# SBUF layout by size, one table for exp and ln, and a 64-byte shift between two weight rings

## The chip, the cores and the metric

The kernel runs on one core of one Trainium2 chip. The metric is the device time of the whole kernel in microseconds (us). The kernel before takes 2155.08 us, the median of 3 runs (2154.45 to 2155.72).

## The reference

The reference is a decoder trunk of two layers over 256 tokens of width 2048, float32. Each layer has a mixer and a feed-forward block:

```python
h = rmsnorm(x, g_norm) @ w_in                       # 2048 -> 3072: q, k, v of 4 + 4 heads of 128
o_sb  = stick_breaking(rmsnorm(qa), rmsnorm(ka), va)
o_dil = dilated_attention(rope(rmsnorm(qb)), rope(rmsnorm(kb)), vb)
x = x + concat([rmsnorm(o_sb), rmsnorm(o_dil)]) @ w_out
x = x + ffn(rmsnorm(x))       # layer 0: dense SwiGLU, d_ff 5632; layer 1: top-2 of 8 experts, 1408 each
```

Stick-breaking attention needs log1p(exp(z)) of the scores and later an exp of the result; dilated attention is a masked softmax, computed here as one softmax with a count per key. So each head needs both exp and ln.

## The kernel before, in words

The 256 tokens are two tiles of 128 (t = 0, 1). Every large product is made of float32r matmuls in three parts. A weight is split in a high part (rounded to float32r) and a low part (the rest), and so is the activation; the product is high x high + high x low + low x high, added up in PSUM. Activations are the stationary operand (128 columns), weights the moving one (mostly 512 columns, 256 in the last gate/up block of a feed-forward slice). The function `three` issues them: L417 has w_high moving, L418 w_low moving, both against the high part of the activation, and L419 has w_high moving against its low part.

Weights arrive in pieces of 128 x 1024 floats (512 KB) through a ring of 11 slots. SyncE loads a piece into raw_pieces (L320) when the slot is free; ScalarE copies it, rounded, to w_high (L748); VectorE writes raw minus high to w_low (L997), which has the same addresses as raw_pieces; TensorE then uses it. ScalarE and VectorE work 6 pieces ahead (LEAD), 14 in the expert stage. There are 96 pieces for w_in and 32 for w_out over both layers, 264 for the dense block and 528 for the experts.

The stages follow one another in each layer. The input projection and the gate and up products have xT_high and xT_low (the normalised, transposed activation) as stationary operands. The output projection and the down products have hT_high and hT_low (the transposed attention output, or the transposed hidden activation). In the expert stage only 128 gathered tokens are used per expert (t = 0 alone); gathers (L659) and scatters (L673, L674, with selection_T stationary) lie among the products.

The order of work on each engine is written out by hand, with semaphores between engines. Between the input and the output projection lies the attention stage, in which no weight piece is used. For each head ScalarE evicts and scales transposed q and k (L810, L811, L814), copies the scores z (L822) and their absolute value (L823), computes exp(-|z|) (L825) and ln(1 + ...) (L826), then exp for the softmax (L829, L830), then exp for the stick-breaking weights (L836). VectorE computes row maxima of the dilated scores (L1133 to L1136), then from the ln the softplus and its masks (L1139 to L1143), then multiplies the softmax terms by the counts (L1146) and sums them (L1148, L1149, L1150), and then forms the exponent of the stick-breaking weights (L1156 to L1158) from TensorE's suffix sums (L500 to L502). In one head VectorE does them in this order, and TensorE the scores of the next head (L484 to L491) after the suffix sums of this one.

ScalarE's functions come from table sets. The program gets a table load (ACT_TABLE_LOAD) ahead of an activation whose function is not in the set that is loaded. exp and ln alternate in every head; sqrt is used before and after the attention stage (L772); Copy, Abs and Square never cause a load here between others.

SBUF tensors are laid out one behind the other in the order in which they are declared; raw_pieces, mixer_scratch and heads_scratch share the addresses of the tensors declared after them. In the kernel before, the order and the bytes per partition are: w_low 45,056; w_high 45,056; x_resid 16,384; token_major 24,576; xT_high 16,384; xT_low 16,384; silu_gate 4096; h_blocks 4096; identity, incl, ones, neg_not_strict, keep_strict 512 each; branch_count and neg_union 1536 each; rope_cos, rope_sin, router_high, router_low 512 each; expert_gates 64; small 256; hT_high 11,264; hT_low 11,264; and behind them small tensors and iota_slots 512, selection 1024, selection_T 1024.

Of the kernel before, what the change touches and what calls it, by code (L numbers as in the profile page):

```python
# [6 lines left out]
F32 = mybir.dt.float32  # L7
F32R = mybir.dt.float32r
# [5 lines left out]
P = 128  # L14
SEQ = 256
TILES = SEQ // P
# [9 lines left out]
FC = FE // P  # L26
# [62 lines left out]
SLOTS = P  # L89
# [34 lines left out]
def trunk(nc, x, positions, norm_mix, w_in, q_norm_sb, k_norm_sb, q_norm_dil, k_norm_dil, out_norm_sb,  # L124
# [36 lines left out]
    with ExitStack() as ctx:  # L161
        def sb(name, shape, dt=F32, where=ctx):
            return where.enter_context(nc.sbuf_tensor(name, shape, dt))
# [4 lines left out]
        with ExitStack() as scratch:  # L168
            RAWS = sb("raw_pieces", [P, RING, PW], F32, scratch)
        WL = sb("w_low", [P, RING, PW], F32R)  # L170
        WH = sb("w_high", [P, RING, PW], F32R)
        X = sb("x_resid", [P, TILES, D])
        TOK = sb("token_major", [P, TILES * D_IN])

# [1 line left out]
            ATT = sb("mixer_scratch", [P, 2 * KD * SEQ], F32, scratch)  # L176
        XTH = sb("xT_high", [P, KD, SEQ], F32R)
        XTL = sb("xT_low", [P, KD, SEQ], F32R)
        SG = sb("silu_gate", [P, 2 * TILES, GW])
        HB = sb("h_blocks", [P, 2, TILES, GW])  # L180
        IDN = sb("identity", [P, P])
# [3 lines left out]
        KEEPZ = sb("keep_strict", [P, P])  # L185
        CNT = sb("branch_count", [P, 3 * P])
        NEGU = sb("neg_union", [P, 3 * P])
        COS = sb("rope_cos", [P, TILES, DH // 2])
        SIN = sb("rope_sin", [P, TILES, DH // 2])
        WRH = sb("router_high", [P, KD, N_EXP], F32R)  # L190
# [3 lines left out]
        XN = TOK[:, 0:TILES * D].rearrange("p (t n) -> p t n", t=TILES)  # L194
        GAIN = TOK[:, TILES * D:TILES * D + D]
        QKV = TOK[:, :].rearrange("p (t n) -> p t n", t=TILES)

        with ExitStack() as scratch:
            PRE = sb("heads_scratch", [P, 2 * FC * SEQ], F32, scratch)
        HTH = sb("hT_high", [P, FC, SEQ], F32R)  # L200
        HTL = sb("hT_low", [P, FC, SEQ], F32R)


        at = [0]
# [26 lines left out]
        SSP = sb("block_square_sums", [P, TILES * DBLOCKS])  # L231
        JUNK = SG[:, :, :].rearrange("p t n -> p (t n)")[:, 0:NB]
        SB_GAIN = SMALL[:, 4:6]
# [7 lines left out]
        R1 = sb("router_rows", [P, 4, TILES, N_EXP])  # L241
        CHOSEN = sb("chosen", [P, TILES, N_EXP])
        SLOT = sb("slot", [P, TILES, N_EXP])
        IOTA = sb("iota_slots", [P, SLOTS])
        SEL = sb("selection", [P, TILES, SLOTS])
        LGT = SEL[:, :, :].rearrange("p t s -> p (t s)")[0:N_EXP, :]
        SELT = sb("selection_T", [P, SEQ], F32R)
        FLAG = sb("another_pass", [P, 1], I32)
        YH = [HTH[:, 4 * i:4 * i + 4, P:2 * P] for i in range(2)]
        YL = [HTL[:, 4 * i:4 * i + 4, P:2 * P] for i in range(2)]  # L250
# [62 lines left out]
        def _(sp):  # L313
# [13 lines left out]
            for t in range(TILES):  # L327
                sp.dma_start(X[:, t, :], x[t * P:(t + 1) * P, :]).then_inc(x_in[t], 16)
            for layer in range(LAYERS):
# [15 lines left out]
            for d in range(DBLOCKS):  # L345
                for t in range(TILES):
                    sp.wait_ge(sc_free, 2 + last + TILES * d + t + 1)
                    sp.dma_start(out[t * P:(t + 1) * P, d * NB:(d + 1) * NB],
                                 X[:, t, d * NB:(d + 1) * NB]).then_inc(stored, 16)
            sp.wait_ge(stored, 16 * DBLOCKS * TILES)  # L350
# [62 lines left out]
        def _(pe):  # L413
# [22 lines left out]
            def both_tiles(banks, act, k, slot, lo, width, first, last):  # L436

                for t in range(TILES):
                    ins = three(banks[t][:, 0:width], act, (slice(None), k, slice(t * P, (t + 1) * P)),
                                (WH, WL), (slice(None), slot, slice(lo, lo + width)), first, last)  # L440
                return ins

            pe.wait_ge(const_done, 1)
            for layer in range(LAYERS):
# [4 lines left out]
                for c in range(IN_BLOCKS):  # L449
# [4 lines left out]
                    for j in range(IN_PIECES):  # L454
                        n = m["p_in"] + c * IN_PIECES + j
                        pe.wait_ge(low_done, n + 1)
                        for u in range(2):
                            k = 2 * j + u
                            ins = both_tiles(PAIR[c % 2], (XTH, XTL), k, n % RING, u * NB, NB, k == 0, k == KD - 1)
                        ins.then_inc(used, 1)  # L460
# [98 lines left out]
                if layer == 1:  # L559
                    pe.wait_ge(wr_done, 1)  # L560
                    for k in range(KD):
                        ks = (slice(None), k, slice(None))
                        ins = three(DN[0][0:N_EXP, 0:SEQ], (WRH, WRL), ks, (XTH, XTL), ks, k == 0, k == KD - 1)
                    ins.then_inc(lgt_ready, 1)
# [7 lines left out]
                def ffn_slice(e):  # L572
# [12 lines left out]
                    for i in range(SLICE_PIECES):  # L585
                        n = f["piece"] + i
                        if i < GU_PIECES:
# [6 lines left out]
                            for k, lo in units:  # L594
                                ins = both_tiles(PAIR[b % 2], (XTH, XTL), k, n % RING, lo, 2 * gu_width(b), k == 0,
                                                 k == KD - 1)
# [29 lines left out]
            def moe_pass(n_pass):  # L626
                s = PASS[n_pass]

                def piece_products(bnk, act, k, slot, lo, width, first, last):
                    return three(bnk[:, 0:width], act, (slice(None), k, slice(0, SLOTS)), (WH, WL),  # L630
                                 (slice(None), slot, slice(lo, lo + width)), first, last)

                def gate_up(e, i):
# [6 lines left out]
                    for k, lo in units:  # L640
                        ins = piece_products(G[b % 2], (XTH, XTL), k, n % RING, lo, 2 * gu_width(b), k == 0, k == KD - 1)
                    ins.then_inc(used, 1)
# [94 lines left out]
        def _(act):  # L737
# [7 lines left out]
            def high(piece, shift=0):  # L745

                act.wait_ge(raw_full[piece % RING], shift * (16 * SLICE_PIECES // RING) + 16 * (piece // RING + 1))
                act.activation(WH[:, piece % RING, :], RAWS[:, piece % RING, :], ACT.Copy).then_inc(high_done, 1)  # L748

            n_square = [0]  # L750

            def squares(d, t):

                act.wait_ge(sq_done, n_square[0]) if n_square[0] else None
                n_square[0] += 1
                act.activation(JUNK, X[:, t, d * NB:(d + 1) * NB], ACT.Square,
                               accum_out=SSP[:, DBLOCKS * t + d:DBLOCKS * t + d + 1]).then_inc(sq_done, 1)
# [21 lines left out]
            for layer in range(LAYERS):  # L779
# [11 lines left out]
                for c in range(IN_BLOCKS):  # L791
# [5 lines left out]
                    if c in QK_BLOCKS:  # L797
                        n = QK_BLOCKS.index(c)
                        roots(HSSR[:, 8 * n:8 * n + 8], ROOTS * layer + 1 + n)

                act.wait_ge(sbg_done, layer + 1)

                def turned(h):
# [182 lines left out]
        def _(dve):  # L986
# [7 lines left out]
            def low(piece, shift=None):  # L994

                dve.wait_ge(high_done, piece + 1 if shift is None else shift * SLICE_PIECES + (piece + 1))
                dve.tensor_tensor(WL[:, piece % RING, :], RAWS[:, piece % RING, :], WH[:, piece % RING, :],  # L997
                                  ALU.subtract).then_inc(low_done, 1)
# [7 lines left out]
            def normalise(norm):  # L1006

                dve.wait_ge(sq_done, X_BLOCKS * (norm + 1))
                link(dve.tensor_reduce(SS, SSP[:, :].rearrange("p (t d) -> p t d", t=TILES), AX.X, ALU.add))
                inverse_roots(RSTD, SS, D, ROOTS * (norm // 2) + (ROOTS - 1) * (norm % 2))  # L1010
                dve.wait_ge(xg_done, X_BLOCKS * (norm + 1))

            def times_gain(d, t):

                cols = slice(d * NB, (d + 1) * NB)
                dve.tensor_tensor(XN[:, t, cols], X[:, t, cols], GAIN[:, cols], ALU.mult).then_inc(xg_done, 1)

# [16 lines left out]
            def x_low(k, t, q):  # L1034
                dve.wait_ge(tp_high, k + 1)
                dst = (slice(None), slice(4 * q, 4 * q + 4), slice(t * P, (t + 1) * P))
                dve.tensor_tensor(XTL[dst], TP[k % 2][:, :].rearrange("p (c n) -> p c n", c=4), XTH[dst],  # L1037
                                  ALU.subtract).then_inc(tp_free, 1)
# [38 lines left out]
            for layer in range(LAYERS):  # L1077
# [17 lines left out]
                def heads_normalised(c):  # L1095
# [5 lines left out]
                    link(dve.tensor_tensor(SQ, cols, cols, ALU.mult))  # L1101
                    link(dve.tensor_reduce(sums, SQ.rearrange("p t (h d) -> p (t h) d", d=DH), AX.X, ALU.add))
                    inverse_roots(rs, sums, DH, ROOTS * layer + 1 + n)
# [175 lines left out]
            def moe_pass(n_pass):  # L1279
# [12 lines left out]
                def gathered_low(high_count, k, q):  # L1292
                    dve.wait_ge(tp_high, high_count + 1)
                    dst = (slice(None), slice(4 * q, 4 * q + 4), slice(0, SLOTS))
                    dve.tensor_tensor(XTL[dst], TP[k % 2][:, :].rearrange("p (c n) -> p c n", c=4), XTH[dst],
                                      ALU.subtract).then_inc(tp_free, 1)
# [131 lines left out]
```

## Time and profile before

| | |
|---|---|
| median of 3 runs | 2155.08 us |
| the profiled execution's own time | 2153.96 us |
| its span in the trace | 2152.2 us |
| TensorE busy | 2036.9 us (95%) |
| VectorE busy | 1426.2 us (66%) |
| ScalarE busy | 1166.0 us (54%) |
| HBM traffic | 492 MB, 229 GB/s over the span |

The profile is of one execution. Matmuls are pipelined and the records of two neighbours overlap, so a busy TensorE is not one at its peak; the distance between the starts of two matmuls is the rate. The granted clock tells which level the throttle allows TensorE: 1.0 is 2.4 GHz, 0.5 is 1.2 GHz. The stages lie, in us from the start of the span, at about: input projection of layer 0 to 166, attention to 221, output projection to 268, dense block 286 to 1053, input projection of layer 1 to 1180, attention to 1233, output projection and routing to 1330, experts to the end.

### The profile page before, as it was taken

To read this page: it belongs to the slowest core of one execution; us is meant where nothing else is said; L and a number is where in the kernel's file an instruction comes from. 1 tells how busy PE (TensorE), PEld (TensorE's weight loads), DVE (VectorE), ACT (ScalarE), POOL (GpSimd) and SP (SyncE) were. 2 spreads that over 40 slices of the span, in tenths; PEclk is the share of its full clock that TensorE was granted. 3 is DMA by queue.
4 is the path that set the end of the run, shared out by engine and by line. 5 is a ranking of instruction groups with operands and counts; after the bars stand their busy time and mean duration, and the time that the engine had idled before them with its cause. 6 is when DMAs were issued, how large, how long until landed. Compare 5 with 4: busy or idle time off the path is not lost.

```text
span 2152.2 us, 28336 instructions
## 1 busy us (share of the span) xinstructions
PE 2036.9 (95%) x9604; PEld 1686.8 (78%) x9604; DVE 1426.2 (66%) x1714; ACT 1166.0 (54%) x1460; POOL 13.5 (1%) x35
## 2 busy tenths in 40 slices
PE   5995989999999999999899688999999999999998
PEld 4884778888888887888687567888888888888886
DVE  7564554544454454446556566888989898989896
ACT  5437443443443443434434734777777776767675
POOL 1000000000000000000000000000000000000000
PEclk9998989999999999999899798999999999999999
DMA  6551445555555555555355044989898998989896
GB/s 226 191 193 39 166 147 187 186 188 194 186 186 189 193 185 187 187 186 188 128 195 186 22 156 159 359 313 347 320 341 322 336 335 320 345 315 354 306 359 251
DMA packets 135270, 493.54 MB, mean 229 GB/s; under 512 B 15264, under 2 KB 15264, under 8 KB 134400
## 3 DMA queue, kind: packets, MB, share of 16 engines
q1 hardware_dynamic: 133920, 486.60, 63.4%
q0 software_dynamic: 1248, 5.61, 0.8%
q8 instruction: 61, 1.00, 0.2%
q14 instruction: 41, 0.34, 0.0%
HBM read 490.05 MB, written 2.10 MB: 229 GB/s over the span
## 4 chain that ended last, share of the span: by engine, by line
PE 91%; ACT 4%; DVE 3%; issue 1%; DMA 0%; DVEq 0%; ACTq 0%; POOLq 0%
PE main L417 28%; PE main L419 28%; PE main L418 28%; PE transpose L659 3%; PE transpose L424 1%; PE spread L673 1%; PE spread L674 1%; DVE xT_low L1037 1%; PE transpose L699 1%; ACT L826 0%; PE transpose L581 0%; DMA token_major<-in_norm_mix 0%; ACT w_high L748 0%; ACT xT_high L767 0%; DVE w_low L997 0%
## 5 line engine op out<-in xcount | busy, mean ns | idle before, releaser
L997 DVE TENSOR_TENSOR w_low<-raw_pieces,w_high 128x1024 fp32r<-128x1024 f32 x920 | 1087.9, 1219 | 432.7 <-ACT w_high L748 420.5
L748 ACT ACTIVATE w_high<-raw_pieces 128x1024 fp32r<-128x1024 f32 x920 | 933.2, 1056 | 259.9 <-DMA raw_pieces<-in_ffn_dense 135.4
L417 PE MATMUL main<-w_high,xT_high 128*128 128x512 f32 (+1 forms) x1920 | 730.3, 380 | 5.5 <-DVE xT_low L1037 4.5
L419 PE MATMUL main<-w_high,xT_low 128*128 128x512 f32 (+1 forms) x1920 | 723.1, 377 | 0.0
L418 PE MATMUL main<-w_low,xT_high 128*128 128x512 f32 (+1 forms) x1920 | 722.7, 376 | 0.0
L417 PEld LDWEIGHTS main<-w_high,xT_high 128*128 128x128 f32 x1920 | 363.0, 189 | 73.1 <-issue 4.3
L419 PEld LDWEIGHTS main<-w_high,xT_low 128*128 128x128 f32 x1920 | 362.8, 189 | 66.3
L418 PEld LDWEIGHTS main<-w_low,xT_high 128*128 128x128 f32 x1920 | 363.4, 189 | 64.1
L417 PE MATMUL main<-w_high,hT_high 128*128 128x512 f32 x832 | 333.8, 401 | 2.8 <-DVE hT_low L1180 2.8
L418 PE MATMUL main<-w_low,hT_high 128*128 128x512 f32 x832 | 329.8, 396 | 0.0
L419 PE MATMUL main<-w_high,hT_low 128*128 128x512 f32 x832 | 329.6, 396 | 0.0
L417 PEld LDWEIGHTS main<-w_high,hT_high 128*128 128x128 f32 x832 | 157.3, 189 | 39.3 <-DVE hT_low L1180 3.6
L419 PEld LDWEIGHTS main<-w_high,hT_low 128*128 128x128 f32 x832 | 156.9, 189 | 38.1
L418 PEld LDWEIGHTS main<-w_low,hT_high 128*128 128x128 f32 x832 | 157.2, 189 | 35.4
L908 ACT ACTIVATE silu_gate<-main 128x256 f32<-128x256 f32 (+1 forms) x48 | 15.0, 364 | 210.3 <-PE main L419 210.3
L1187 DVE TENSOR_TENSOR x_resid<-main,x_resid 128x512 f32<-128x512 f32 x48 | 31.9, 687 | 120.6 <-PE main L419 120.6
L424 PE MATMUL transpose<-identity,token_major 128*128 128x128 f32 x160 | 40.5, 424 | 56.7 <-DVE token_major L1021 31.0
L424 PEld LDWEIGHTS transpose<-identity,token_major 128*128 128x128 f32 x160 | 29.2, 216 | 67.5 <-issue 29.1
L954 ACT ACTIVATE hT_high<-main 128x512 fp32r<-128x512 f32 x32 | 19.2, 599 | 100.2 <-PE main L419 100.2
L796 ACT ACTIVATE token_major<-main 128x512 f32<-128x512 f32 x24 | 13.0, 595 | 100.6 <-PE main L419 100.6
L659 PEld LDWEIGHTS transpose<-selection,token_major 128*128 128x128 f32 x512 | 63.8, 198 | 4.2 <-DVEq L1240 1.6
L659 PE MATMUL transpose<-selection,token_major 128*128 128x128 f32 x512 | 64.2, 281 | 1.6 <-DVEq L1240 1.6
(203 smaller groups left out, 883.4 us busy)
## 6 DMA issues: line engine op xcount, KB each, us to landing
raw_pieces<-in_ffn_moe SPq DMA_DIRECT2D x528, 512.0 KB, 5.1
raw_pieces<-in_ffn_dense SPq DMA_DIRECT2D x264, 512.0 KB, 3.4
raw_pieces<-in_w_in SPq DMA_DIRECT2D x96, 512.0 KB, 4.3
raw_pieces<-in_w_out SPq DMA_DIRECT2D x32, 512.0 KB, 4.2
x_resid<-in_x SPq DMA_DIRECT2D x2, 1024.0 KB, 7.0
token_major<-in_norm_mix POOLq DMA_DIRECT2D x2, 1024.0 KB, 7.2
token_major<-in_norm_ffn POOLq DMA_DIRECT2D x2, 1024.0 KB, 5.0
out_x<-x_resid SPq DMA_DIRECT2D x8, 256.0 KB, 2.7
```

The costliest lines, as they stand in the source:

```text
L417: pe.matmul(out_ap, lh[ls], rh[rs], start=first, stop=False)
L418: pe.matmul(out_ap, lh[ls], rl[rs], start=False, stop=False)
L419: return pe.matmul(out_ap, ll[ls], rh[rs], start=False, stop=last)
L424: ins = pe.transpose(TP[k % 2][:, i * P:(i + 1) * P], src[:, c * P:(c + 1) * P], IDN[:, :])
L659: ins = pe.matmul(TP[k % 2][:, i * P:(i + 1) * P], XN[:, t, c * P:(c + 1) * P], SEL[:, t, :], start=t == 0, stop=t == TILES - 1)
L673: pe.matmul(bnk, rows, YH[d % 2], start=True, stop=False)
L674: pe.matmul(bnk, rows, YL[d % 2], start=False, stop=True).then_inc(sc_ready, 1)
L699: ins = pe.transpose(TP[n % 2][:, c * P:(c + 1) * P], HB[:, b % 2, 0, c * P:(c + 1) * P], IDN[:, :])
L748: act.activation(WH[:, piece % RING, :], RAWS[:, piece % RING, :], ACT.Copy).then_inc(high_done, 1)
L997: dve.tensor_tensor(WL[:, piece % RING, :], RAWS[:, piece % RING, :], WH[:, piece % RING, :], ALU.subtract).then_inc(low_done, 1)
L1037: dve.tensor_tensor(XTL[dst], TP[k % 2][:, :].rearrange("p (c n) -> p c n", c=4), XTH[dst], ALU.subtract).then_inc(tp_free, 1)
L1187: dve.tensor_tensor(xs, PAIR[d % 2][t][:, :], xs, ALU.add).then_inc(dn_free, 1)
```

## The change

It does three things. Large SBUF tensors (hT, and the selection tensors) are declared ahead of the small ones. A pad of 64 bytes stands between w_low and w_high, and one of 448 bytes behind w_high. And ahead of each attention stage ScalarE loads one table set, named natural_log_exp_and_others. Nothing else of the program changes.

```diff
         WL = sb("w_low", [P, RING, PW], F32R)
+        PAD = sb("ring_shift", [P, P // 8])
         WH = sb("w_high", [P, RING, PW], F32R)
+        PAD2 = sb("ring_shift_back", [P, P - P // 8])
         X = sb("x_resid", [P, TILES, D])
...
         XTL = sb("xT_low", [P, KD, SEQ], F32R)
+        with ExitStack() as scratch:
+            PRE = sb("heads_scratch", [P, 2 * FC * SEQ], F32, scratch)
+        HTH = sb("hT_high", [P, FC, SEQ], F32R)
+        HTL = sb("hT_low", [P, FC, SEQ], F32R)
         SG = sb("silu_gate", [P, 2 * TILES, GW])
...
         NEGU = sb("neg_union", [P, 3 * P])
+        SEL = sb("selection", [P, TILES, SLOTS])
+        SELT = sb("selection_T", [P, SEQ], F32R)
+        IOTA = sb("iota_slots", [P, SLOTS])
         COS = sb("rope_cos", [P, TILES, DH // 2])
...
-        with ExitStack() as scratch:
-            PRE = sb("heads_scratch", [P, 2 * FC * SEQ], F32, scratch)
-        HTH = sb("hT_high", [P, FC, SEQ], F32R)
-        HTL = sb("hT_low", [P, FC, SEQ], F32R)
...
-        IOTA = sb("iota_slots", [P, SLOTS])
-        SEL = sb("selection", [P, TILES, SLOTS])
         LGT = SEL[:, :, :].rearrange("p t s -> p (t s)")[0:N_EXP, :]
-        SELT = sb("selection_T", [P, SEQ], F32R)
...
                         roots(HSSR[:, 8 * n:8 * n + 8], ROOTS * layer + 1 + n)
 
+                act.preload_act_table_set("natural_log_exp_and_others")
                 act.wait_ge(sbg_done, layer + 1)
```

## Rows read from the trace of the kernel before

**Rows 1.** The page: busy time by engine, and the chain's shares by engine.
```profile
PE 2036.9 (95%) x9604; PEld 1686.8 (78%) x9604; DVE 1426.2 (66%) x1714; ACT 1166.0 (54%) x1460; POOL 13.5 (1%) x35
...
PE 91%; ACT 4%; DVE 3%; issue 1%; DMA 0%; DVEq 0%; ACTq 0%; POOLq 0%
```

**Rows 2.** TensorE's waits, 1345 to 2140: us in total, times, longest.
```profile
PE transpose L699 <- DVE h_blocks L1322: 2.5, 8, 0.3
```

**Rows 3.** The windows view: stretch, us, busy (instructions) per engine, PEclk, DMA share, GB/s.
```profile
1345.00:2140.00 795.00, 792.47 (x3905) 661.17 (x3904) 695.37 (x744) 567.78 (x655) 0.00 (x0) 1.00 0.91 332
```

**Rows 4.** Timeline of TensorE, xT stationary: start us, us, engine, line, operation. 26 rows between.
```profile
157.70 0.39 PE L418 MATMUL main<-w_low,xT_high 128*128 128x512 f32 x1
...
163.82 0.39 PE L418 MATMUL main<-w_low,xT_high 128*128 128x512 f32 x1
```

**Rows 5.** The same, hT stationary: output projection (28 rows between), experts (9 between).
```profile
228.15 0.40 PE L418 MATMUL main<-w_low,hT_high 128*128 128x512 f32 x1
...
234.92 0.39 PE L417 MATMUL main<-w_high,hT_high 128*128 128x512 f32 x1
...
1484.19 0.40 PE L418 MATMUL main<-w_low,hT_high 128*128 128x512 f32 x1
...
1486.53 0.40 PE L419 MATMUL main<-w_high,hT_low 128*128 128x512 f32 x1
```

**Rows 6.** The page's groups: counts of L417, with xT and with hT.
```profile
L417 PE MATMUL main<-w_high,xT_high 128*128 128x512 f32 (+1 forms) x1920 | 730.3, 380 | 5.5 <-DVE xT_low L1037 4.5
...
L417 PE MATMUL main<-w_high,hT_high 128*128 128x512 f32 x832 | 333.8, 401 | 2.8 <-DVE hT_low L1180 2.8
```

**Rows 7.** Timeline of TensorE at 1.2 GHz, right after attention. Three rows between.
```profile
222.19 0.63 PE L418 MATMUL main<-w_low,hT_high 128*128 128x512 f32 x1
...
223.89 0.63 PE L419 MATMUL main<-w_high,hT_low 128*128 128x512 f32 x1
```

**Rows 8.** Timeline of ScalarE, head 0 of layer 0.
```profile
165.84 1.08 ACT L796 ACTIVATE token_major<-main 128x512 f32<-128x512 f32 x2 [8.15 <-PE main L419]
166.81 0.48 ACT L810 ACTIVATE mixer_scratch<-transpose,small 128x256 f32<-128x256 f32 x1
...
169.55 1.28 ACT L825 ACT_TABLE_LOAD   x1
```

**Rows 9.** L1139's waits in 8 heads (us, times), and timeline rows of VectorE and ScalarE.
```profile
  ACT mixer_scratch L826: 13.0, 8
...
182.75 0.56 DVE L1139 SCALAR_TENSOR_TENSOR mixer_scratch<-mixer_scratch 128x384 f32<-128x384 f32 x1 [0.84 <-ACT mixer_scratch L826]
...
184.34 0.49 ACT L830 ACTIVATE mixer_scratch<-mixer_scratch,small 128x256 f32<-128x256 f32 x1
184.54 0.28 DVE L1143 TENSOR_TENSOR mixer_scratch<-mixer_scratch,keep_strict 128x128 f32<-128x128 f32 x1
...
1192.65 0.56 DVE L1139 SCALAR_TENSOR_TENSOR mixer_scratch<-mixer_scratch 128x384 f32<-128x384 f32 x1 [0.66 <-ACT mixer_scratch L826]
...
1210.35 0.56 DVE L1139 SCALAR_TENSOR_TENSOR mixer_scratch<-mixer_scratch 128x384 f32<-128x384 f32 x1 [0.93 <-ACT mixer_scratch L826]
```

**Rows 10.** Groups of ScalarE: table loads in attention, count | busy us, mean ns | idle before.
```profile
L826 ACT ACT_TABLE_LOAD x8 | 10.3, 1283 | 0.1
L829 ACT ACT_TABLE_LOAD x8 | 10.3, 1283 | 0.1
...
L825 ACT ACT_TABLE_LOAD x2 | 2.6, 1283 | 0.0
```

**Rows 11.** Timeline of TensorE, 256 columns: router (3 rows between), then main (19 between).
```profile
1299.83 0.28 PE L418 MATMUL main<-xT_low,router_high 128*8 128x256 f32 x1
...
1300.30 0.28 PE L419 MATMUL main<-xT_high,router_low 128*8 128x256 f32 x1
...
1479.79 0.28 PE L417 MATMUL main<-w_high,xT_high 128*128 128x256 f32 x1
...
1482.19 0.28 PE L419 MATMUL main<-w_high,xT_low 128*128 128x256 f32 x1
```

## The prediction

> **What bounds the kernel now.** I read the page's busy shares and chain first. TensorE is busy for 2036.9 of 2152.2 us and carries 91% of the chain that ended last; ScalarE has 4% of it and VectorE 3% [rows 1]. So only two things can move the end: how fast TensorE goes through its matmuls, and the stretches in which it does nothing. The waits of TensorE in the expert stage (1345 to 2140) come next: 2.5 us in 795 [rows 2]. This stage moves the most bytes, but the DMA share is 0.91 at 332 GB/s [rows 3], and TensorE never waits there for a weight piece. The kernel is TensorE-bound from end to end, outside the two attention stages.
>
> Since matmuls overlap, their mean duration says nothing of the rate; the distance from one start to the next does, so the timeline is the view that matters. With xT as the stationary operand, 27 matmuls of 512 columns go by between 157.70 and 163.82: 6.12/27 = 226.7 ns each [rows 4]. With hT as the stationary operand, in the output projection, 29 go by between 228.15 and 234.92: 233.4 ns; in the expert stage 10 between 1484.19 and 1486.53: 234 ns [rows 5]. Shape, width, clock level (2.4 GHz, granted clock 1.0) and moving operand (w_high, w_low) are the same. At 2.4 GHz, 512 columns alone are 213.3 ns, so each matmul carries 13.4 ns (xT) or 20 ns (hT) on top. While the clock was granted at 1.2 GHz, four took 1.70 us, 425 ns each [rows 7], which is 512 columns and nothing on top.
>
> **What the layout may have to do with it.** By the allocation order and sizes of the kernel before, and counting from w_low, w_high lies 45,056 bytes further, xT_high 131,072, xT_low 147,456: all whole multiples of 512 bytes. hT_high comes after two small tensors of 64 and 256 bytes and lies 180,032 bytes after w_low, which is 351 x 512 + 320; hT_low has the same remainder. A slice of 128 columns is 512 bytes, a ring slot 4096, so the remainder holds for every operand of these matmuls. This remainder is the one thing in which I find hT to differ from xT, in two stages with different loops, and in both the distance is 6.7 ns greater. I take it as the cause. Both rows come with the weight load of the next matmul beside the running one, so I read the excess as the two reads getting into each other's way.
>
> The Trainium skill (TensorE: Matmul & The Clock Gate, the pipeline's first step, LDWEIGHTS) says that TensorE has two independent SBUF read ports and that loading the next weights doesn't steal read bandwidth from the running matmul. By that rule the layout is worth nothing. The trace speaks against it: the same instruction forms go at two rates. I go by the trace and keep the rule's outcome as rival C.
>
> **Part 1, the layout by size.** hT_high, hT_low, selection, selection_T and iota_slots move ahead of the small tensors. With both pads together 512 bytes, x_resid, token_major and xT keep their remainder of 0, and hT_high gets it too: it lies 163,840 + 512 = 164,352 bytes after w_low, 321 x 512. No instruction is added or removed. The stationary hT then stands to w_low as xT does, and I take xT's distance for it: 3 x 832 = 2496 matmuls [rows 6] x (233.3 - 226.7 = 6.6 ns) = 16.5 us, all on TensorE and so all on the path. Bounds: 0, if the remainder is not the cause; the saving could be larger if selection_T, whose remainder becomes 0 too, speeds up the 128 scatter matmuls (at 7 ns, under 1 us). DMA hides none of it: of the 832 groups of three, 352 are in the expert stage, so some 7 us of its 795 go, and the DMA share of 0.91 would rise by 0.01.
>
> **Part 2, the 64-byte shift.** All of w_high, the moving operand of L417 and L419 (two of every three matmuls), now has remainder 64, while w_low and all stationary operands have 0. No row of before shows a remainder of 64. On the low side there is a bound: the router's matmuls of 256 columns with only 8 stationary columns to load go 0.47/4 = 117.5 ns apart, against 2.40/20 = 120 ns for the main ones of that width [rows 11], so some 2.5 ns per matmul are what a whole weight load costs beyond a nearly empty one. If the shift took that away from all 3 x (1920 + 832) = 8256 matmuls, it would give 20.6 us. Above: if remainder 64 is as bad as 320, L417 and L419 pay 6.6 ns: 5504 x 6.6 = 36.3 us lost. The far end, no excess at all as at 1.2 GHz, would be 8256 x 13.4 = 110 us; nothing at 2.4 GHz comes near it. The splits on ScalarE and VectorE also read and write the rings; TensorE doesn't wait for them, so a small change in them is hidden by TensorE's own time. I take 0 between 20.6 gained and 36.3 lost, since rows give no sign, and the zero is the weakest term of the sum.
>
> **Part 3, one table.** Table loads of 1283 ns: 8 at L826 (ln), 8 at L829 (back to exp), 2 at L825 (exp after the square root) [rows 10]. With a set holding both functions all 18 go, and 2 come, ahead of the wait on sbg_done. Is the new load hidden? No: ScalarE's two evictions run to 166.92 and L810 starts at once (166.81, the two overlap a little); the load pushes L810, the score matmuls and all after it back by 1.28 us. It takes the place of the load at 169.55, which was on the chain as well [rows 8]. These cancel: 0 (bounds: 1.28 us each way, per layer).
>
> The load at L826 stands before the ln whose result L1139 waits for. VectorE's idle time before L1139 is 13.0 us in 8 heads; removing a load gives at most 1.28 us of each wait. Three waits are shorter, 0.84, 0.66 and 0.93 [rows 9], because VectorE's row-maximum work, which comes after TensorE's scores, ends later than the ln without its load would; the other five give 1.28. Sum 5 x 1.28 + 2.43 = 8.8 us. The load at L829 feeds L1146 by way of L830. In head 1 of layer 0 VectorE starts L1139 at 182.75 and is busy until L1143 ends at 184.82; L830 ends at 184.83 [rows 9]. Both arrive together, so removing this load alone gives nothing: VectorE's five operations are late next. Worth 0 (bounds: 0 and 8 x 1.28 = 10.3 us). Behind it, ScalarE's evictions come earlier, but no one is late for them. In the same rows the instruction after a load starts 0.01 us after its end: the Trainium skill (ScalarE: Activation LUTs, What ACT_TABLE_LOAD costs) adds a drain of 1380 ns to each switch; the trace doesn't show it. With it the part would be worth about twice as much.
>
> TensorE's clock: the granted clock is 1.2 GHz at times in the attention stages and for six matmuls after them [rows 7]. Shorter idle time may shift these stretches either way; six matmuls at 1.2 GHz cost 6 x 0.2 = 1.2 us, so I allow 2 us each way.
>
> **The sum**, on the profiled execution (2153.96 us, 1.76 more than its span): -16.5 + 0 - 8.8 = -25.3, so 2128.7; the median of the runs is 1.1 us above it: 2129.8. I say 2130.
>
> **Rivals.**
> A, the forecast: rings as now, hT as xT: 2130. Its own range is 2119 to 2139 (the clock, part of a shift gain, a part of hT's excess that stays).
> B, the shift costs. Two of three matmuls get hT's 6.6 ns: -25.3 + 36.3 = +11: 2166. For it: hT, 320 bytes off, shows that a ring and a stationary operand at unequal remainders can be slow; a shift makes L417 and L419 unequal. If the reads repeat over 128 bytes, 320 and 64 are the same thing. Against: three matmuls in a row may settle otherwise than when all have one remainder. The result turns slower once the shift costs more than 25.3/5504 = 4.6 ns per shifted matmul.
> C, layout without effect (the two rates have another cause): 2155.1 - 8.8 = 2146. Against: two stages, same difference.
> D, the shift helps: up to 20.6 us more, 2109. For it: reads that start in different places need not meet. Then the expert stage would come closer to DMA: its share of 0.91 at 332 GB/s would rise by about the same part as TensorE gets faster, under 2%, so the end still follows TensorE.
> E, the table pass still loads for ln or exp: 8.8 us less gain, 2139, or 2155 with C.
>
> **How the numbers follow.** A 0.45, B 0.22, C 0.10, D 0.18, E 0.05. The time is A's. Range 2109 to 2164: it takes in D almost whole, A, C, E and the milder half of B; outside it remain a B at full price or worse and a D beyond its bound, together about 0.18. About 0.2% (4.3 us) is what a measurement of this kernel can tell. Faster: A, C, D, E and a mild B, 0.80; within 0.2%: 0.04; slower: 0.16.
>
> **What would show it.** Starts of matmuls with hT 226.7 ns apart instead of 233.4 confirm part 1; 233.4 unchanged mean C. With xT: 226.7 is A, less is D, 231 on average over a group of three is B. Table loads at L825, L826 and L829 gone, one per layer ahead of L810, idle before L1139 down from 13.0 to about 4 us confirm part 3; loads at L826 still there mean E. The forecast is wrong if xT's distance moves by over 2 ns either way.

## The result, and the profile after

The changed kernel takes 2168.68 us (median of 6 runs, 2166.31 to 2172.36) against 2154.17 us for the kernel before (6 runs): ratio 1.0068, 95% interval 1.0055 to 1.0081. It is slower by 14.5 us, where 2130 was forecast. Rival B, the shift that costs, had been worked out at 2166. Every ratio in this document is to the kernel before as run beside the other kernel, and one execution stands in no ratio: of the three of e5_shift_128 one took 10,066.52 us, while the others took 2142.95 and 2143.90.

The distances between matmul starts tell it. These are timeline rows of TensorE in the changed kernel (start us, us, engine, line), with xT stationary; 23 rows lie between the first and the last. They answer to [rows 4]; `three` is one line further down, L418 to L420, since a line was added above it.

```profile
99.71 0.40 PE L418 MATMUL main<-w_high,xT_high 128*128 128x512 f32 x1
99.94 0.40 PE L419 MATMUL main<-w_low,xT_high 128*128 128x512 f32 x1
100.18 0.39 PE L420 MATMUL main<-w_high,xT_low 128*128 128x512 f32 x1
...
105.31 0.40 PE L418 MATMUL main<-w_high,xT_high 128*128 128x512 f32 x1
```

5.60/24 = 233.3 ns, where it was 226.7. With hT stationary, in the output projection (23 rows between), answering to [rows 5]:

```profile
231.63 0.40 PE L418 MATMUL main<-w_high,hT_high 128*128 128x512 f32 x1
...
237.23 0.40 PE L418 MATMUL main<-w_high,hT_high 128*128 128x512 f32 x1
```

Again 5.60/24 = 233.3 ns, as before. So xT got slower and hT gained next to nothing: its mean distance is 233.4 ns in the dense block, 232.6 in the experts and 231.0 in the second output projection, where it was 233.3 in all of them. The page shows the busy shares of [rows 1] hardly changed, and the table loads of ScalarE (groups: count, busy us, mean ns, idle before) are what part 3 promised: the 18 of [rows 10] are gone, and two stand at L802.

```profile
PE 2060.9 (95%) x9604; PEld 1684.4 (78%) x9604; DVE 1426.7 (66%) x1714; ACT 1145.1 (53%) x1444; POOL 13.5 (1%) x35
...
PE 92%; DVE 4%; ACT 3%; issue 1%; DMA 0%; DVEq 0%; ACTq 0%; POOLq 0%
```

```profile
L802 ACT ACT_TABLE_LOAD x2 | 2.6, 1283 | 0.0
```

The table below is worked out from the starts of the first and the last main matmul of each stage (us; attention from the last xT matmul to the first hT one; the last line counts matmuls of every kind). Two experiments, told below, stand beside the two kernels.

| stage | before | after | e1_no_shift | e2_table_only |
|---|---|---|---|---|
| input projection, layer 0 | 132.1 | 137.0 | 132.5 | 131.9 |
| attention, layer 0 | 56.2 | 50.1 | 51.1 | 51.4 |
| output projection, layer 0 | 46.0 | 46.1 | 45.8 | 46.5 |
| dense block | 742.3 | 752.7 | 735.0 | 739.7 |
| input projection, layer 1 | 132.5 | 136.3 | 132.1 | 132.5 |
| attention, layer 1 | 55.8 | 48.6 | 51.3 | 51.5 |
| output projection, layer 1 | 46.4 | 46.0 | 45.5 | 46.8 |
| experts | 824.6 | 834.2 | 819.6 | 824.6 |
| norms, routing, end | 92.4 | 92.6 | 93.8 | 92.6 |
| first to last matmul | 2128.3 | 2143.6 | 2106.7 | 2117.5 |

Before to after: the stages with weight matmuls take 28.4 us more, the attention stages 13.2 us less. The extra time is xT's: 4992 matmuls of 512 columns at some 6.1 ns more are 30 us; the 768 of 256 columns went the other way, from 119.8 to 118.8 ns, 0.8 us less. TensorE still does not wait for weights in the expert stage (1345 to 2140; us in total, times, longest), as in [rows 2]:

```profile
PE transpose L700 <- DVE h_blocks L1324: 2.6, 8, 0.3
```

### The profile page after: what moved, and what is told of

Read it like the earlier page. It is cut to its first block, busy times and chain, and to the rows that moved or that the text cites. A ratio compares the mean times of both kernels' runs of the same rounds, so it can differ in the third digit from the quotient of the medians.

```text
span 2166.9 us, 28320 instructions
## 1 busy us (share of the span) xinstructions
PE 2060.9 (95%) x9604; PEld 1684.4 (78%) x9604; DVE 1426.7 (66%) x1714; ACT 1145.1 (53%) x1444; POOL 13.5 (1%) x35
## 4 chain that ended last, share of the span: by engine, by line
PE 92%; DVE 4%; ACT 3%; issue 1%; DMA 0%; DVEq 0%; ACTq 0%; POOLq 0%
PE main L418 28%; PE main L419 28%; PE main L420 28%; PE transpose L660 3%; PE transpose L425 1%; PE spread L674 1%; PE spread L675 1%; DVE xT_low L1039 1%; PE transpose L700 1%; PE transpose L582 0%; DMA token_major<-in_norm_mix 0%; ACT w_high L749 0%; ACT xT_high L768 0%; DVE w_low L999 0%; DVE token_major L1018 0%
## 5 line engine op out<-in xcount | busy, mean ns | idle before, releaser
L749 ACT ACTIVATE w_high<-raw_pieces 128x1024 fp32r<-128x1024 f32 x920 | 933.4, 1056 | 265.5 <-DMA raw_pieces<-in_ffn_dense 137.7
L418 PE MATMUL main<-w_high,xT_high 128*128 128x512 f32 (+1 forms) x1920 | 741.9, 386 | 4.7 <-DVE xT_low L1039 4.5
L419 PE MATMUL main<-w_low,xT_high 128*128 128x512 f32 (+1 forms) x1920 | 735.0, 383 | 0.0
L420 PE MATMUL main<-w_high,xT_low 128*128 128x512 f32 (+1 forms) x1920 | 729.3, 380 | 0.0
L418 PEld LDWEIGHTS main<-w_high,xT_high 128*128 128x128 f32 x1920 | 361.4, 188 | 82.7 <-DVE xT_low L1039 3.6
L420 PEld LDWEIGHTS main<-w_high,xT_low 128*128 128x128 f32 x1920 | 364.1, 190 | 75.4
L419 PEld LDWEIGHTS main<-w_low,xT_high 128*128 128x128 f32 x1920 | 363.7, 189 | 71.9
L418 PE MATMUL main<-w_high,hT_high 128*128 128x512 f32 x832 | 334.6, 402 | 2.8 <-DVE hT_low L1182 2.8
L419 PE MATMUL main<-w_low,hT_high 128*128 128x512 f32 x832 | 330.4, 397 | 0.0
L420 PE MATMUL main<-w_high,hT_low 128*128 128x512 f32 x832 | 328.5, 395 | 0.0
L418 PEld LDWEIGHTS main<-w_high,hT_high 128*128 128x128 f32 x832 | 156.9, 189 | 39.5 <-DVE hT_low L1182 3.6
L420 PEld LDWEIGHTS main<-w_high,hT_low 128*128 128x128 f32 x832 | 157.6, 189 | 37.4
L419 PEld LDWEIGHTS main<-w_low,hT_high 128*128 128x128 f32 x832 | 157.5, 189 | 34.7
```

Of the source, the lines that this page charges most:

```text
L418: pe.matmul(out_ap, lh[ls], rh[rs], start=first, stop=False)
L419: pe.matmul(out_ap, lh[ls], rl[rs], start=False, stop=False)
L420: return pe.matmul(out_ap, ll[ls], rh[rs], start=False, stop=last)
```

## The experiments

**The change taken apart.** Four kernels: the changed kernel without its pads, and each of the three parts alone on the kernel before.

```diff
 e1_no_shift, against the changed kernel; e4_layout_only also drops the preload
-        PAD = sb("ring_shift", [P, P // 8])
-        PAD2 = sb("ring_shift_back", [P, P - P // 8])
 e2_table_only, against the kernel before
+                act.preload_act_table_set("natural_log_exp_and_others")
                 act.wait_ge(sbg_done, layer + 1)
 e3_shift_only, against the kernel before
+        PAD = sb("ring_shift", [P, P // 8])
         WH = sb("w_high", [P, RING, PW], F32R)
+        PAD2 = sb("ring_shift_back", [P, P - P // 8])
```

> The changed kernel without its two pads: layout by size and the one table stay. Theory 1 (the forecast's mechanism for hT, and the shift as the cost): every operand has remainder 0, so matmuls start 226.7 ns apart with xT and with hT alike; 2154 - 13 (attention stages, as in the changed kernel) - 16.5 (hT) = about 2125 us. Rival 2 (hT's 233.3 ns is not from its remainder): hT stays at 233.3 ns, 2141 us. Rival 3 (the slow xT comes from the moved tensors, not from the shift): xT stays at 233.3 ns, about 2167 us.

Measured: 2129.45 us (4 runs, 2128.02 to 2131.77), ratio 0.9885 (0.9869 to 0.9902). The timeline of TensorE, xT and then hT stationary, with 23 rows between in each pair:

```profile
109.76 0.39 PE L417 MATMUL main<-w_low,xT_high 128*128 128x512 f32 x1
...
115.20 0.39 PE L417 MATMUL main<-w_low,xT_high 128*128 128x512 f32 x1
...
235.67 0.39 PE L416 MATMUL main<-w_high,hT_high 128*128 128x512 f32 x1
...
241.11 0.39 PE L416 MATMUL main<-w_high,hT_high 128*128 128x512 f32 x1
```

5.44/24 = 226.7 ns in both. Theory 1 holds in the distances, rivals 2 and 3 fall: hT's extra time did come from its place, and xT's new slowness comes from the pads. The total is 4 us above theory 1's 2125, which had counted on the 13 us that the changed kernel gained in the attention stages; here these are 9.6 us shorter than before. This is the version that beats both kernels, by 24 us and 39 us.

> The kernel before with the one table load per layer alone. Theory 1 (the table is worth more than the 8.8 us of the forecast, because TensorE's clock in the attention stages recovers too): the two attention stages get 13 us shorter together, 2141 us, and xT and hT stay at 226.7 and 233.3 ns. Rival 2 (part of the 13 us comes from the layout, by way of the attention stages' own reads): 8.8 us, 2145 us.

Measured: 2142.31 us, ratio 0.9946 (0.9930 to 0.9963). xT stays at 226.7 ns, hT at 233.3. The two attention stages are 9.0 us shorter together, from 111.9 to 102.9. That is rival 2's number for the attention stages, and the forecast's 8.8, not theory 1's 13. Rival 2's reason is not shown by it: e1_no_shift has the layout too, and its attention stages take 102.4. Of the 11.5 us in the medians another 2.5 are in the dense block, where no instruction changed. The starts in the two traces tell where. The block begins at 1.2 GHz, for 5.7 us before and 3.2 here (granted clock of its first 10 us: 0.72 and 0.84), and after 15 matmuls 1.1 us of the difference is there. The other 1.4 us are three steps at the ends of its slices, where hT gives way to xT: before, the largest steps from start to start there are 0.68 and 1.08 us, here none is over 0.45. Why the clock rose earlier and the pauses went is open; no edit lies near them. The changed kernel's further 4 us in attention are taken up below.

> The kernel before with the two pads alone (w_high at remainder 64, hT at 320 as before, two tables as before). Theory 1 (the shift costs xT 6.6 ns and the attention stages nothing): xT at 233.3 ns, + 29 us in the input projections, gate and up products; hT stands to w_high at another remainder, which nobody has measured: if it stays at 233.3 ns, 2183 us; if it moves to the fast value, 2167 us. Rival 3 (the slow xT comes from the moved tensors): xT at 226.7 ns, 2154 us.

Measured: 2173.90 us, ratio 1.0091 (1.0074 to 1.0108). xT: mean distances of 231.1 ns in the first input projection and 233.3 in the dense block, the second projection and the experts; hT 229.1 in both layers' output projection and 230.4 in the experts. Neither of theory 1's totals came (2183 and 2167), since hT went to neither of its two values. The shift costs by itself; with hT at remainder 320 it even helps hT by 4 ns, so that what counts is a relation between two operands and not the remainder of one. This fits what the next experiments find: w_high then stands 64 - 320 = -256 bytes from hT, and only w_low is still at -320. The parts don't add up either: layout, table and shift alone make -10.9, -11.5 and +20.1 us, together -2.3, where the changed kernel with all three has +14.5. On the layout of before the shift slows xT and speeds hT up; on the layout by size it slows both.

> The kernel before with the layout by size alone. Theory 1: xT and hT at 226.7 ns, two tables in attention: 2154 - 16.5 = 2137.5 us. Rival 2 (remainders don't matter for hT): 2154 us.

Measured: 2142.94 us, ratio 0.9948 (0.9932 to 0.9965). hT at 226.9 ns, the attention stages as long as before (56.3 us each). The layout alone gives 10.9 us, against 16.5 in the expectation: the distances are as expected in every stage, but some stretches give part of it back (the input projections are 1.4 us longer together and the routing 1.0), and in the experts hT's mean is 227.6, since each gather and scatter between the down products disturbs the row for a few matmuls.

**Which relation counts.** Eight more kernels, all with the layout by size and the one table. By the relation of a matmul is meant the place of its moving operand minus the place of its stationary one, in bytes.

```diff
 e5_shift_128, e6_shift_256, e7_shift_32: the changed kernel with other pads, 512 bytes together
-        PAD = sb("ring_shift", [P, P // 8])
+        PAD = sb("ring_shift", [P, 32])        # 64 in e6, 8 in e7
-        PAD2 = sb("ring_shift_back", [P, P - P // 8])
+        PAD2 = sb("ring_shift_back", [P, 96])  # 64 in e6, 120 in e7
 e8_both_64: PAD of 16 floats ahead of raw_pieces and w_low instead of between the rings
 e9_both_192 and e10_both_128: the same with 48 and 32 floats (PAD2 of 80 and 96)
 e11_act_low_64, against e1_no_shift, and the same for HTL (the two scratch tensors get 128 floats more);
 e12_act_low_128 with 32 and 96
+        PAD = sb("low_shift", [P, 16])
         XTL = sb("xT_low", [P, KD, SEQ], F32R)
+        PAD2 = sb("low_shift_back", [P, 112])
```

> The changed kernel with w_high shifted by 128 instead of 64 bytes (and 384 behind it). Theory 1a (the reads meet by their place within 128 bytes): as without a shift, 226.7 ns with xT and hT, about 2130 us. Theory 1b (by their place within 512 bytes): another distance than 226.7 ns, up to hT's 233.3 ns and 2168 us.

> The same with 256 bytes. Theory 1a: 226.7 ns, 2130 us. Theory 1b: another distance; if the two reads are now as far from each other as they can be, a shorter one, down to 224 ns, 2108 us.

> The same with 32 bytes. If whole 64-byte lines count (theory 1a), 32 bytes lie in the same line at the start but cross into the next one in the middle of each: between 226.7 and 233.3 ns, some 230 ns, 2149 us. If only shifts of a whole 64 bytes matter: 226.7 ns, 2130 us.

> Both rings shifted by 64 bytes against the activations, and so equal among themselves; 448 bytes behind w_high. Theory A (what counts is moving against stationary operand, as hT with 320 bytes shows): 233.3 ns with xT and hT, 2166 us. Rival (what counts is w_high against w_low, whose reads follow one another): 226.7 ns, 2130 us.

> Both rings shifted by 192 bytes against the activations (320 behind them). Moving minus stationary is then 192, which modulo 256 is the relation that hT has in the kernel before (0 - 320 = -320 = 192 modulo 256). Theory P (the place within 256 bytes, moving against stationary, sets the distance): 233.3 ns with xT and hT alike, the rest as e1_no_shift, 2129 + 5760 x 6.6 ns + 2496 x 6.6 ns = about 2183 us, less if the 256-column ones gain as in the run before. Rival (that both rings are shifted doesn't matter, 64 bytes cost by the start of the ring): 229 ns as with both at 64, 2143 us.

> The same with 128 bytes, half of the 256 after which the shift of w_high alone came back to 226.7 ns. Theory P1 (two reads half the period apart meet least): below 226.7 ns, down to 224, 2108 us. Theory P2 (the fast value is the floor, and remainders other than 0 only add): between 226.7 and 233.3 ns, 2130 to 2183 us.

> Rings unshifted; the low halves of the activations (xT_low, hT_low, the stationary operands of one matmul in three) 64 bytes further. Theory P2: one relation in three leaves 0, so 226.7 ns rises to between 228 and 231 ns, 2140 to 2165 us. Theory P1' (a stagger can help when only one of three has it): below 226.7 ns, under 2125 us.

> The same with 128 bytes. Theory P2: as with w_high shifted by 128 (229 ns), but for one matmul in three: 227.5 to 229 ns, 2133 to 2143 us. Theory P1': below 226.7 ns, under 2125 us.

Measured, with the mean distance in the dense block (512 columns, xT and hT):

| kernel | moving minus stationary, bytes | xT ns | hT ns | us | ratio (95%) |
|---|---|---|---|---|---|
| e1_no_shift | 0 | 227.0 | 226.9 | 2129.45 | 0.9885 (0.9869 to 0.9902) |
| e6_shift_256 | w_high 256, w_low 0 | 227.0 | 226.9 | 2131.73 | 0.9892 (0.9864 to 0.9921) |
| e5_shift_128 | w_high 128, w_low 0 | 229.0 | 228.9 | 2143.90 | 0.9950 (0.9922 to 0.9979) |
| e8_both_64 | both 64 | 229.0 | 229.0 | 2143.38 | 0.9950 (0.9928 to 0.9973) |
| e11_act_low_64 | w_high against the low activation -64, the others 0 | 231.0 | 231.1 | 2154.75 | 1.0001 (0.9990 to 1.0013) |
| e12_act_low_128 | w_high against the low activation -128, the others 0 | 231.2 | 231.2 | 2157.06 | 1.0013 (1.0001 to 1.0024) |
| e7_shift_32 | w_high 32, w_low 0 | 231.2 | 231.1 | 2156.58 | 1.0014 (1.0003 to 1.0025) |
| e10_both_128 | both 128 | 232.5 | 232.4 | 2165.91 | 1.0055 (1.0032 to 1.0078) |
| the changed kernel | w_high 64, w_low 0 | 233.3 | 233.4 | 2168.68 | 1.0068 (1.0055 to 1.0081) |
| e9_both_192 | both 192 | 233.3 | 233.3 | 2169.69 | 1.0076 (1.0047 to 1.0106) |

One pair of rows each (xT stationary, 23 rows between) shows the fast and the slow end of the table, e6_shift_256 and then e9_both_192:

```profile
109.81 0.39 PE L418 MATMUL main<-w_high,xT_high 128*128 128x512 f32 x1
...
115.25 0.39 PE L418 MATMUL main<-w_high,xT_high 128*128 128x512 f32 x1
```

```profile
109.72 0.39 PE L420 MATMUL main<-w_high,xT_low 128*128 128x512 f32 x1
...
115.32 0.39 PE L420 MATMUL main<-w_high,xT_low 128*128 128x512 f32 x1
```

5.44/24 = 226.7 ns and 5.60/24 = 233.3 ns. What follows:
- A shift of w_high by 256 bytes gives what 0 gives, one of 128 doesn't (229.0 ns). Both have 512 bytes of pads like the changed kernel, so it is not the pads' size. Theory 1a, a period of 128 bytes, falls; nor does 1b's further hope, that the largest distance is the best, hold. A shift of 32 bytes gives 231.2 ns, where some 230 had been expected, and is slower than one of 128: the cost doesn't grow with the shift.
- e9 puts xT into the relation that hT has in the kernel before (0 - 320 = -320, which is 192 modulo 256), and xT takes hT's 233.3 ns. It takes hT's rhythm too: by the starts in the traces, xT's distances here and hT's before mostly alternate between 236 and 231 ns, where the changed kernel reaches the same mean as 232, 233, 240, 230, 234 and 231. So it is more than two slow values that happen to agree. Together with e1 and e4 this makes the places of the moving and the stationary operand relative to each other the cause of [rows 5]. What was not run is a kernel with rings and activations all shifted alike, which by this should be as fast as e1. The expected total of 2183 was 13 us too high: it put 6.6 ns on the 768 matmuls of 256 columns too, and they went from 119.8 down to 115.5 ns, which makes 8.4 us of it.
- e8 rules out its rival in its strict form: two equal rings are not enough, they must stand right to the activations. Its expected 233.3 ns was wrong too: both at 64 give 229.0 and not what both at 192 give. The relation is not symmetric.
- Theories P1 and P1', that some stagger does better than 0, fall for every shift in the table; 0 and 256 are the best, for matmuls of 512 columns. P2, that other relations only add, holds, and e10 and e11 came within its ranges. One was missed: e12 was expected at 227.5 to 229 ns and 2133 to 2143 us and came at 231.2 ns and 2157.06 us. One matmul in three at -128 costs more than two in three at 128 (229.0 ns, e5).
- With one of the three matmuls of a group off 0 (e11), the mean over the group is 231.0 ns (229, 229 and 236 in the starts of the input projection), 13 ns more for the three; with all three off by 64 the other way it is 229.0, 7 ns more. So the costs of single matmuls don't add up. Nor does the relation of each matmul say it all: -64 is 192 modulo 256, and with w_low alone at that relation (e3, hT in the output projections) the mean is 229.1 ns, with w_high against the low activation alone at it (e11) 231.0.

## Why the prediction was wrong, step by step

**What bounds the kernel: right.** TensorE alone set the end outside attention. Most of each change of the distances showed up in the stages' times, in the experts too: 1920 xT matmuls at 5.6 ns more and 1056 hT matmuls at 0.7 ns less make 10.0 us there, and the stage took 9.6 us more, with the DMA share at 0.93 instead of 0.91.

**Part 1, the layout: right in itself.** "The stationary hT then stands to w_low as xT does, and I take xT's distance for it" holds in e1 (226.7 ns) and e4. Worth: dense block and experts 7.3 and 5.0 us shorter than before in e1; against e2, which differs from e1 by the layout alone, the total is 12.9 us less in the medians (2142.31 - 2129.45), where 16.5 was forecast. In the dense block the distances alone would give 1056 x 6.5 ns = 6.9 us and the stage got 4.7 us shorter (739.7 to 735.0); 0.5 us of the rest are in its start, which is 1.2 us longer at 1.2 GHz, and 1.4 us in pauses at the ends of three slices, 0.58 to 0.94 us from start to start. Rival C is out: the same instructions had distances 2.3 to 6.6 ns longer, by nothing but addresses. The Trainium skill (TensorE: Matmul & The Clock Gate, the step LDWEIGHTS) says that loading the next weights takes nothing from the running matmul's reads; the outcome worked out from it, that a layout is worth nothing, is not what these runs show. That the two reads get into each other's way, as the prediction read the excess, is not shown either: the runs show that their places matter, not how.

**Part 2, the shift: the step that failed.** "I take 0 between 20.6 gained and 36.3 lost, since rows give no sign". The shift costs 39.2 us in the medians (2168.68 - 2129.45), 36.9 us between the first and the last matmul. The upper bound of 36.3, "if remainder 64 is as bad as 320", was near the truth by luck: it counted 5504 shifted matmuls at 6.6 ns each. And 64 and 320 are not the same thing, as rival B supposed for a period of 128 bytes: both rings at 64 give 229.0 ns, hT's relation gives 233.3. What happens is that the whole group of three slows down, the matmul with the unshifted w_low (L419 in the changed kernel) included: of the distances 232, 233, 240, 230, 234 and 231 ns the largest is one from L419 to L420. Against e1 that is 7488 matmuls of 512 columns at some 6.0 ns, 45 us, less 1 us for the 256-column ones and 3.7 us in attention; another 3 us are given back at the stages' edges, in pauses between slices and in the routing. There was a sign in the rows, and the text named it under rival B: among the weight matmuls hT in [rows 5] was the one with unequal places, and it was slow. Two relations had been measured there, 0 and one other, and 0 was the better. To hold that a third leaves things as they are was the optimistic reading; with it at "slow", the sum would have given 2166.

**Part 3, one table: right, and more on top in the changed kernel.** Loads gone and added as forecast; the new one is on the path in front of L812 and takes the place of the old one at L825. Timeline of ScalarE after, answering to [rows 8]:

```profile
170.61 1.09 ACT L797 ACTIVATE token_major<-main 128x512 f32<-128x512 f32 x2 [9.48 <-PE main L420]
171.72 1.28 ACT L802 ACT_TABLE_LOAD   x1
173.01 0.47 ACT L812 ACTIVATE mixer_scratch<-transpose,small 128x256 f32<-128x256 f32 x1
```

VectorE's idle time before the softplus (L1141 now), which the forecast let fall from 13.0 to about 4 us, is 4.0 us in 4 waits; this is the row of the waits view that answers to the first of [rows 9]:

```profile
DVE mixer_scratch L1141 <- ACT mixer_scratch L828: 4.0, 4, 1.0
```

e2 shows 9.0 us for this part in the attention stages, forecast 8.8. The same step from e4 to e1, on the layout by size, gives 10.3 us (112.65 to 102.38), so the match to 0.2 us is closer than the forecast could know. The zero for the load at L829 and the zero for the new load were not tried one by one. The drain of 1380 ns that the Trainium skill (ScalarE: Activation LUTs, What ACT_TABLE_LOAD costs) adds to a switch is not in the rows above either: the load starts 0.02 us after the eviction in front of it ends, and L812 0.01 us after the load.

In the changed kernel the attention stages are 13.2 us shorter, 4 more, with the same instructions as in e1 and e2. The windows view (granted clock and DMA share behind the busy times) shows the difference in TensorE's clock, one kernel after the other: the changed kernel, e2_table_only, e1_no_shift, each 54 us from about the end of the input projection.

```profile
168.00:222.00 54.00, 32.36 (x180) 27.23 (x179) 28.12 (x74) 33.85 (x76) 1.59 (x3) 0.79 0.12 40
1190.00:1244.00 54.00, 34.19 (x180) 28.61 (x181) 31.27 (x77) 34.76 (x76) 0.53 (x1) 0.81 0.14 46
```

```profile
165.00:219.00 54.00, 33.78 (x173) 28.40 (x172) 27.97 (x74) 34.26 (x77) 1.60 (x3) 0.73 0.12 40
1176.00:1230.00 54.00, 37.23 (x175) 31.50 (x176) 30.42 (x72) 29.65 (x66) 0.54 (x1) 0.74 0.10 35
```

```profile
165.00:219.00 54.00, 34.36 (x175) 29.19 (x174) 27.98 (x74) 34.35 (x77) 1.60 (x3) 0.74 0.12 41
1170.00:1224.00 54.00, 36.17 (x177) 30.04 (x176) 31.44 (x76) 30.51 (x68) 0.54 (x1) 0.77 0.10 34
```

The granted clock is 0.79 and 0.81 in the changed kernel against 0.73 to 0.77 in the others, so TensorE spent less of the stage at 1.2 GHz. Suffix sums and scores are on the path there, at half speed while the clock is low. The forecast allowed 2 us each way for this; it was 4. The other kernels with one table bear it out. The time at 1.2 GHz in the two stages (from their length and granted clock) and their length go together: 37.3 us and 98.7 us in the changed kernel, 40.6 and 100.1 in e7, 45.1 and 102.1 in e8, 48.5 and 102.4 in e1, 52.6 and 102.9 in e2. Why the low stretches fall otherwise when the stage starts some us later is open. No run changed the clock alone.

**Chances.** A had 0.45 and B 0.22. After e1 it can be said that A was right for the kernel without the pads (2129.45 measured, 2130 forecast), and that one step, the shift, made the whole difference. That A came within 1 us there is partly luck: the layout gave 12.9 us instead of 16.5, and the table 11.5 in the medians instead of 8.8. A's sign of being wrong did come: xT's distance moved by 6.6 ns, where over 2 was the limit.

## What to carry to other kernels

When TensorE is the bound, read the distance between matmul starts and compare it between stages with the same instruction forms; a difference of a few ns in 8000 matmuls is tens of microseconds, and the cause may be where the stationary operand lies relative to the moving one. Here, keeping all operands of a kind of matmul at the same place modulo 256 bytes (declare the large tensors before the small ones) gave the shortest distance for 512 columns, and no stagger that was tried did better. A cost with no row for its sign should be taken as the nearest rows have it: the one unequal relation in the trace was slow, and so was the new one.

## What was not expected of the hardware

- The distance of float32r matmuls of 512 columns at 2.4 GHz took values between 226.7 and 233.3 ns by addresses alone, with 512/2.4 = 213.3 ns in none of the stages; at 1.2 GHz it was 0.43 us in the shifted kernels too, as this pair from e8_both_64 shows, two matmuls apart (0.86/2), the same as the 425 ns of [rows 7] within the rounding of the view:

```profile
1223.08 0.63 PE L419 MATMUL main<-w_low,hT_high 128*128 128x512 f32 x1
...
1223.94 0.63 PE L418 MATMUL main<-w_high,hT_high 128*128 128x512 f32 x1
```

- The distances settle into short repeating patterns, and the same addresses can have two: e8_both_64 has 229.1 ns with hT in layer 0 and 233.3 in layer 1, e3_shift_only 231.1 and 233.3 ns with xT in the two input projections, e7_shift_32 233.4 and 231.1. Transposes or a stretch at 1.2 GHz lie in front of each. With the relation of 0 the mean stayed between 226.7 and 227.7 ns in every stage.
- Matmuls of 256 columns are ordered otherwise: 119.8 ns on average without a shift, 118.8 in the changed kernel, and 115.5 in e9_both_192, the slowest for 512 columns.
- What meets what (a memory bank, a buffer, the order of the two reads) no run shows. The period of 256 bytes rests on one shift of 256 against three smaller ones of w_high (32, 64, 128), on e9's agreement with hT's 320, and on hT's gain in e3_shift_only.
